# Half of the value chunks on another DMA queue, two loads later in their queue, and one evacuation earlier: a decoder step on one Trainium2 core

## What is computed

```python
# retention, per head h (4 heads of 256)
o, s_new = retention_seq(rotary(q), rotary(k) * 256 ** -0.5, v, s0)   # chunks of 128
o = (o - mean(o)) * rsqrt(var(o) + eps) * ret_norm_g
b = silu(gate) * o

# peer, per token: 8 heads, 16 experts each, chosen out of 16384
u = take(peer_u, expert); a = gelu(u . x)
y = sum over heads and experts of (g * a) * take(peer_v, expert)
```

## Time and profile before

| | before |
|---|---|
| median of 3 runs | 4537.35 us (4532.19 to 4538.72) |
| the profiled execution's own time | 4544.36 us |
| its span, first to last instruction | 4542.6 us |
| PE busy | 4381.2 us, 96% of the span |
| POOL, DVE, ACT busy | 61%, 48%, 34% |
| mean granted clock | 0.989 |
| quads with up and down part | from about 2763 to 4377 us of the span |

### The profile page before, as it was taken

The page is one execution under the profiler, slowest core; times in us unless marked ns, Lnnn a source line. Parts: engine busy times, 40 slices in busy tenths (PEclk is TensorE's granted clock), DMA queues, the critical chain, the costliest instruction groups (busy, mean ns, idle before and its releaser), DMA issues.

```text
span 4542.6 us, 75520 instructions
## 1 busy us (share of the span) xinstructions
PE 4381.2 (96%) x28787; PEld 4141.9 (91%) x28787; DVE 2177.9 (48%) x3231; ACT 1525.1 (34%) x1921; POOL 2774.2 (61%) x1440
## 2 busy tenths in 40 slices
PE   7999999999999989999999998999999999999998
PEld 7899989899888978888888998999999999999998
DVE  3132333423102153333333565777777777777656
ACT  4422222222222244444443553333333333333332
POOL 6833222243222457777777887788788788886643
PEclk9999999999999999999999999999999999999999
DMA  6643333434564255555555559999999899999854
GB/s 228 209 95 100 111 111 106 155 105 146 196 203 168 88 177 183 182 182 181 181 181 183 187 188 341 350 359 353 354 355 358 320 357 363 358 356 347 324 190 157
DMA packets 493934, 1032.09 MB, mean 227 GB/s; under 512 B 55776, under 2 KB 285280, under 8 KB 461024
## 3 DMA queue, kind: packets, MB, share of 16 engines
q1 hardware_dynamic: 316528, 592.77, 39.9%
q0 software_dynamic: 45056, 268.60, 15.2%
q10 hardware_dynamic: 132208, 168.75, 10.7%
HBM read 935.26 MB, written 94.73 MB: 227 GB/s over the span
## 4 chain that ended last, share of the span: by engine, by line
PE 49%; issue 24%; POOL 17%; DMA 6%; ACT 2%; DVE 1%; POOLq 0%; ACTq 0%; SPq 0%; DVEq 0%
PE PS L598 21%; PE PS L948 15%; POOL WS L484 14%; PE PS L1045 12%; DMA RAW<-in_vE 6%; POOL AR L507 2%; ACT WS L1080 1%; POOL ROWS L517 1%; PE PS L974 0%; DMA ROWS<-in_vE,AR 0%; DMA AR<-gel 0%; DVE AR L1759 0%; DVE AR L2266 0%; PE PS L1001 0%; DVE HL L1782 0%
## 5 line engine op out<-in xcount | busy, mean ns | idle before, releaser
L598 PE MATMUL PS<-HL,WS 128*128 128x288 f32 (+2 forms) x16896 | 2394.9, 303 | 66.6 <-POOL WS L484 35.2
L598 PEld LDWEIGHTS PS<-HL,WS 128*128 128x128 f32 x16896 | 2351.7, 190 | 87.3 <-issue 30.5
L484 POOL TENSOR_TENSOR WS<-RAW,WS 128x1024 fp32r<-128x1024 f32 x600 | 1458.0, 2439 | 1418.8 <-ACT WS L1080 1416.5
L1080 ACT ACTIVATE WS<-RAW 128x1024 fp32r<-128x1024 f32 x600 | 614.8, 1055 | 1190.1 <-PE PS L598 451.6
L1045 PE MATMUL PS<-WW,WS 128*128 128x320 f32 x6144 | 927.0, 312 | 56.5 <-POOL WS L484 44.8
L1045 PEld LDWEIGHTS PS<-WW,WS 128*128 128x128 f32 x6144 | 908.6, 189 | 73.6 <-issue 36.1
L948 PE MATMUL PS<-WS,HL 128*128 128x512 f32 x3072 | 700.4, 389 | 0.0
L948 PEld LDWEIGHTS PS<-WS,HL 128*128 128x128 f32 x3072 | 575.5, 188 | 118.8
L484 POOL TENSOR_TENSOR WS<-CS,WS 128x1024 fp32r<-128x1024 f32 x200 | 482.7, 2414 | 146.9 <-ACT WS L1080 145.1
L2135 DVE SCALAR_TENSOR_TENSOR PS<-ROWS,AR,PS 128x2048 f32<-128x2048 f32 x206 | 483.3, 2346 | 9.0 <-DMA ROWS<-in_vE,AR 8.7
L2150 DVE TENSOR_TENSOR AR<-AR,PS 128x320 f32<-128x320 f32 x512 | 247.1, 483 | 317.9 <-PE PS L1045 316.7
(11 more groups left out here) (220 smaller groups left out, 2274.0 us busy)
## 6 DMA issues: line engine op xcount, KB each, us to landing
RAW<-in_uT SPq DMA_DIRECT2D x256, 512.0 KB, 4.6
RAW<-in_w_lin SPq DMA_DIRECT2D x216, 512.0 KB, 3.6
CS<-in_uT SPq DMA_DIRECT2D x128, 512.0 KB, 4.7
AR<-in_uT SPq DMA_DIRECT2D x128, 512.0 KB
RAW<-in_vE SPq DMA_DIRECT2D x128, 512.0 KB, 7.9
CS<-in_vE SPq DMA_DIRECT2D x64, 512.0 KB, 4.8
AR<-in_vE SPq DMA_DIRECT2D x64, 512.0 KB
AR<-in_w_lin SPq DMA_DIRECT2D x48, 512.0 KB, 4.2
```

Of the source, the lines that this page charges most:

```text
L484: pool.tensor_tensor(WS[:, k, 1, :], raw(k, many, late), WS[:, k, 0, :].bitcast(F32), ALU.subtract)\
L598: ins = mm(to, WS[:, slot + hf, wp, k * P:(k + 1) * P], x, start=first and (wp, xp) == (0, 0), stop=last and wp == 1, skip_group_check=True)
L1080: copy = lambda out, in_, **kw: act.activation(out, in_, ACT.Identity, **kw)
```

## The change

It has three parts. (1) In quads 0 to 26, down chunks 9, 11, 13 and 15 are issued on ACT's queue (`load_odd`) and no longer on SP's: 9 in block (0,1) of `ups` before its gelu, 11 and 13 in block (1,1) before its gelu, 15 behind the last block. Each waits on ACT for the same low part as before on SP. (2) `load_next(i + 1)`, that is the two transfers of 640 KB, stands behind `load_odd(i, 15)` and no longer behind block (1,0), in quads 1 to 25. (3) `evac_head(h + 1, 0)` stands behind the root of the variance of head h, ahead of the wait for `b_done` and the stores; that of head 0 stands ahead of the retention loop, before the 9 loads.

```diff
-            def load_v(i, i12, i4, first):
+            def load_v(i, i12, i4, first, parts=(0, 1)):
                 for q in range(4):
-                    for b in range(2):
+                    for b in parts:
...
-                load_v(i, i * 12, i * 4, 8)
+                load_v(i, i * 12, i * 4, 8, (0,))
...
                 for b in range(SB):
                     act.dma_start(SST[:, b], sret[b, bass.ds(h, 1)]...)
-                evac_head(h, 0)
                 act.wait_ge(S["vt_done"], h + 1)
...
                 act.activation(RSD, RVAR, ACT.Sqrt).then_inc(S["rsd_ready"], 1)
+                if more:
+                    evac_head(h + 1, 0)
                 if not more:
                     store_states(h, 4, SB)
                 act.wait_ge(S["b_done"], h + 2)
...
             act.wait_ge(S["out_a"], 16 * GROUPS)
+            evac_head(0, 0)
             with act.Fori(0, RH - 1) as h:
                 retention(h, True)
...
+            def load_odd(i, k):
+                if k == 9 or k == 13:
+                    act.wait_ge(S["split_done"], split_uv(i * 12, k - 4))
+                else:
+                    act.wait_ge(S["low_done"], low_uv(i * 4, k - 4))
+                q = (k - 9) // 2
+                act.dma_start(raw(k % 4, True, True).rearrange("p (e d) -> p e d", e=2),
+                              vE[bass.ds(i * 4 + 2, 2), :, 512 * q:512 * (q + 1)].rearrange("e p d -> p e d"))\
+                    .then_inc(S[f"raw{k % 4}"], 16)
+
-            def ups(i, first=False):
+            def ups(i, first=False, last_up=False):
...
+                        if (a, e) == (0, 1):
+                            load_odd(i, 9)
+                        if (a, e) == (1, 1):
+                            load_odd(i, 11)
+                            load_odd(i, 13)
                         gelu_out(r + a, n + (4 * a + 2 * e), e)
                         store_gelu(r + a, m + (2 * a + e), e)
...
-                        if (a, e) == (1, 0) and not first:
+                        if (a, e) == (1, 0) and last_up:
                             load_next(i + 1)
+                load_odd(i, 15)
+                if not first and not last_up:
+                    load_next(i + 1)
...
-            ups(QT - 1)
+            ups(QT - 1, last_up=True)
```

## The result

The changed kernel took 4555.23 us (median of 6 runs, 4552.91 to 4566.64) beside 4535.84 us for the kernel before on the same chip (6 runs, 4532.19 to 4538.72): a ratio of 1.0049, 95% interval 1.0036 to 1.0062. Forecast were 4513.5 us and a gain. Both are outside of what was said: the time lies above the range, and the sign is the other one. The profiled execution's own time is 4553.29 us, its span 4551.5. Three executions of the kernel before among those beside the first four experiments (5365 to 6674 us, at a granted clock of 0.60 to 0.75) were slow ones and stand in no median and no ratio here.

A forecast was written before the change was run, and what follows sets the result against it. PE, busy 96% of the span, was held by waits for POOL's low parts. Quads -13.8, clock -4.6, first quad +3 and heads -8.35 sum to -23.8 us, from 4537.35 to 4513.6, stated as 4513.5; range 4500 to 4535.

The forecast's parts named there:

- The step that failed: Quads, chunk 11 on ACT's queue: issued about 2.5 us later, without 1.31 MB beside it; no cost in the sum.
- covered by 1.2 us: Quads, chunks 11 and 13: high copies end by t0 + 3.0, DVE takes low 11 at t0 + 4.2.
- The mechanism of part 2: Quads: 1.31 MB of loads ahead of chunks 12 and 13 delay them; moving the loads ends step 2's waits, 29.6 us.
- The clock term: Three of the last quads: without long waits before step 2 the clock does not fall, -4.6 us.
- The delay of the copy of chunk 12 by the issues: Quads, ACT: copy begins 0.43 us late, step 2 waits 0.63, 15.8 us in 25 quads, leaving -13.8.
- covered, only just: Quads, chunk 9 on ACT: copies and low 6 go 1.0 to 1.2 us later; POOL's 1.24 us idle covers it.
- -8.35: Retention heads: the earlier evacuation removes block 2's waits of 2.58, 3.82 and 1.95 us, all 8.35 us.
- The first quad, +3: First quad: chunks 9, 11, 13, 15 join ACT's queue choked with map stores, +3 us, range 0 to +8.
- Slower: ACT is stopped by its own issues: Rival, quads: a full queue makes ACT's issues long, delaying the copy of chunk 12; 4550 us, chance 0.12.
- Given back: Rival, quads: with DMA engines full, rows or chunks 14 to 1 become late instead; 4532 us, chance 0.15.
- the list of signs: Trace signs of right or wrong; one wrong sign: a transfer appears as releaser at chunk 11, 14 or DVE's rows; unpriced.

The follow-up runs named there:

- the first four experiments: Kernel before with only part 3, 4528.26 us; only part 2, 4506.71; only part 1, 4828.55; changed kernel with chunk 11 on SP, 4507.66.
- the fourth run: Changed kernel, but chunk 11 issued by SP again, between chunks 10 and 12: 4507.66 us, 0.9928 of the kernel before.
- the row earlier: Changed kernel, but POOL issues each quad's fifth row gather behind low 5 and not low 6: 4502.92 us, 0.9912 of the kernel before.
- part 2 alone: Kernel before, all chunks on SP, with only the two 640 KB loads moved behind a wait for low 11: 4506.71 us, 0.9922 of before.
- the rows ahead: Kernel before with parts 2 and 3, and two row gathers issued ahead of low 8 and low 12: 4463.03 us, 0.9823 of before.
- part 3 alone: Kernel before with only each head's first evacuation put ahead of the stores: 4528.26 us, 0.9967 of before.

## Why the prediction was wrong

**The step that failed.** "Chunk 11 itself is issued about 2.5 us later than on SP, without the 1.31 MB beside it." The first half was right: it is 2.8 us later (t0 - 6.4 for - 9.2), about 1 because low 7 ends later behind chunk 9's wait (on SP's queue, in the fourth run, it goes out at - 8.25), and about 2 because the issue now stands behind the copies of block (1,0). The second half was an argument and no price: in the sum the delay stood at nothing. I let the bytes that had gone pay for it, and did not look at what else moves then. It cost 9.6 to 16.5 us from issue to copy where 8.3 would have done. In the DMA answer of the changed quad for 2962 to 2977, the time in which chunk 11 moved (queue: packets, MB, share of 16 engines):

```profile
DMA packets 1606, 5.18 MB, mean 345 GB/s; under 512 B 154, under 2 KB 282, under 8 KB 1231
## 3 DMA queue, kind: packets, MB, share of 16 engines
q0 software_dynamic: 458, 3.07, 54.8%
q1 hardware_dynamic: 517, 0.99, 22.6%
q10 hardware_dynamic: 631, 1.11, 19.8%
```

q0 carries the gathers, q1 the chunks from SP, q10 ACT's: the gathers take 3.07 of 5.18 MB, and ACT's queue is left with 1.11 MB in 15 us, 74 GB/s, of which chunk 11 is half. The 3 us behind its issue show the start of it. These are the same answers before (quad at 3107.40), with chunk 11 a block earlier (quad at 3080.33) and in the change, for 3098.18 to 3101.18, 3071.97 to 3074.97 and 2963.40 to 2966.40:

```profile
q1 hardware_dynamic: 415, 0.81, 77.2%
q0 software_dynamic: 4, 0.00, 0.1%
...
q1 hardware_dynamic: 260, 0.50, 54.4%
q10 hardware_dynamic: 128, 0.26, 26.7%
...
q0 software_dynamic: 96, 0.78, 78.7%
q10 hardware_dynamic: 1, 0.00, 0.1%
```

The fifth row is issued ahead of chunk 11 in all three, by 1.1 us in the first two and by 3.0 in the change, but its packets begin only later: the first five have started 4.5 and 4.6 us behind the issue in the first two, and 3.0 in the change (medians of the quads). So before, and a block earlier, chunk 11 has over 3 us ahead of them, and in the change it meets them at its issue and moves one packet in 3 us. And what it has left at t0 then moves beside the next two rows (issued at 2966.28 and 2969.82). A chunk is 256 packets of 2 KB. By the trace's packet records, 163 to 235 of them had started by t0 in the 23 quads whose copy waits, 244 and 256 in the two untouched ones, and 252 to 256 in all 25 with the row earlier.

The cover that I had counted, "covered by 1.2 us", was that of the copies behind ACT's wait, and not that of the transfer. With that the chain that I had seen for chunk 12 came at chunk 11, where DVE's in-order queue carries it to PE inside the steps.

**The other steps.**

- The mechanism of part 2: right, and shown twice. Without part 1 it gives 35 us by the runs and 28.7 by the quads of the two traces (1447.7 us for 1476.4), where its steps give 29.2 (24.6 + 4.6 of clock). The clock term was right too in this pair of traces: in the quads PE's busy time fell by 5.1 us (1430.98 to 1425.88) with as many waits for POOL.
- The delay of the copy of chunk 12 by the issues, 0.43 us, a wait of 0.63: right in the run with chunk 11 on SP (7.95 and 0.72 in the quad shown). At 10.8 us it was the whole price of part 1 in the sum for quads 1 to 25, a sixth of the 64 us that part 1 cost.
- Chunk 9, "covered, only just": the wait before step 0 stayed 0.62. But it made low 7 and all that hangs on it about 1 us later, chunk 11 too. Covered against PE is not covered against the next issue.
- Part 3: right in its mechanism; -8.35 was mis-sized, it is 11 to 15 us.
- The first quad, +3: wrong in its sign. PE waits 6.97 us (6.84 before) ahead of the down part, but from t0 of quad 0 to t0 of quad 1 it is 62.9 to 64.7 us in the five traces with part 1, and 66.4 to 68.1 in the five without it: it gains 2 to 5 us. Why was not looked into.
- The rivals. "Slower: ACT is stopped by its own issues" has nearly the time that came (4550), but by luck: its cause did not come. The issues of the two loads take 0.35 and 0.38 us in the median, and 0.9 at most. "Given back" named the right kind of cause, a chunk that becomes late instead, but argued it for the rows and chunks 14 to 1, behind the moved loads; the list of signs has a transfer that appears at 11, and this is the sign that came, without a price on it.

Chunk 11's transfer swings between 8.3 us or less and 16.5 us from quad to quad at nearly the same issue time. Whether it ends in time goes with what is left of it at t0; how late it is does not (with 163 packets started its copy began at t0 + 4.5, with 235 at + 7.5). What makes it so, and why the row's packets start earlier in the change, was not found.

## What to carry to other kernels

When a transfer is issued later, price its landing anew: which transfers are in the air at the new time, and what share they leave it. Bytes taken away elsewhere are no answer to that. And follow each moved wait to the next issue on its chain, not only to the engine that is the bound; here 1 us of "covered" delay and 2 us of program order put one chunk behind the packets of a 1 MB gather, and that turned a gain of 33 us into a loss of 19. Of a change in several parts, try each alone: two of these three are worth 45 us without the third.

## What the runs showed of the hardware

- Transfers in the air at the same time share unequally. The row gathers, in packets of 8 KB, moved 3.07 MB in 15 us while the two queues of chunks, in packets of 2 KB, had 0.99 and 1.11. A chunk of 512 KB took 13.9 us beside them, and at most 6.5 us when the fifth row had gone ahead. The three queues moved about as many packets in that stretch (458, 517 and 631). That the packet size is the reason for the unequal bytes was not tested.
- A gather issued first does not move first. With chunk 11 a block earlier it is issued 1.1 us behind the fifth row, and ACT's queue moves 0.26 MB in the 3 us behind its issue while the gathers' queue moves nothing; the first five packets of the row have started 4.6 us behind its issue (median).
- At nearly the same issue time (t0 - 8.25 and - 8.36) SP's and ACT's queue served chunk 11 alike.
- A wait of PE costs more than its length. From t0 of quad 1 to t0 of quad 26 the waits of the change and of the version with chunk 11 on SP differ by 33.5 us and PE's busy time by 14.5 (1441.15 and 1426.67), for the same products. Part of it is no matter of the clock: between part 2 alone and the rows ahead, both at a granted clock of 1.00 throughout the quads, it is 17.3 us of waits and 11.1 of busy time (1425.88 and 1414.78).
- The length of a wait does not tell whether the clock falls. Before, the 1.90 us ahead of 4179.94 left a granted clock of 0.59 for the next 4 us; the 2.88 us ahead of 3533.86 and the 1.86 ahead of 4120.58 left 1.00. And it changes from run to run: three quads had such a fall before, six in the trace of part 3 alone, whose quads have the same code.
